# Two blocks of a fused fp32 transformer kernel: an earlier transpose, a first operand pair split in two, a last output in two parts

## The reference

```python
for i in range(2):
    mod = (c_act @ mod_w[i] + mod_b[i])           # six vectors of 1024
    hin = x * (1 + mod[1]) + mod[0]
    y = mla_mixer(hin) if i == 0 else moba_mixer(hin)
    x = layer_norm(ALPHA * x + mod[2] * y)
    hin = x * (1 + mod[4]) + mod[3]
    y = conv_ffn(hin)                             # 1024 -> 2 x 2816 -> 1024
    x = layer_norm(ALPHA * x + mod[5] * y)
```

## Time and profile before

| | |
|---|---|
| median of 3 runs | 892.44 us |
| profiled execution | 892.48 us |
| its span, first to last instruction | 890.6 us |
| TensorE matmuls | 857.5 us busy, 5768 instructions |
| VectorE | 668.7 us busy, 1090 instructions |
| ScalarE | 452.5 us busy, 720 instructions |
| GpSimd | 68.0 us busy, 62 instructions |
| mean granted TensorE clock | 0.997 |

### The profile page before, as it was taken

How to read it: one execution, slowest core, us unless ns; L and a number is a source line. 1 busy time by engine, 2 the same in 40 slices (tenths; PEclk the granted TensorE clock), 3 DMA queues, 4 the chain that set the end, 5 groups by cost and what they waited for, 6 DMA issues and landing times.

```text
span 890.6 us, 14511 instructions
## 1 busy us (share of the span) xinstructions
PE 857.5 (96%) x5768; PEld 754.0 (85%) x5768; DVE 668.7 (75%) x1090; ACT 452.5 (51%) x720; POOL 68.0 (8%) x62
## 2 busy tenths in 40 slices
PE   8999989999999999999999999899999999999996
PEld 8988978767876898699999999579987899999995
DVE  5598798878976997789757857796777876556557
ACT  5564554454546545275544545265563664444450
POOL 1000001000001120011200100110000111001011
PEclk9999999999999999999999999999999999999999
DMA  9756666555965780799866896389717886646601
GB/s 342 291 165 192 206 234 219 189 165 196 346 222 233 251 293 1 316 332 380 286 228 216 284 351 238 99 268 332 230 47 287 295 300 198 205 164 190 190 1 48
DMA packets 57028, 201.00 MB, mean 226 GB/s; under 512 B 6600, under 2 KB 7936, under 8 KB 56960
## 3 DMA queue, kind: packets, MB, share of 16 engines
q1 hardware_dynamic: 55952, 196.89, 63.2%
q0 software_dynamic: 1008, 3.18, 1.2%
HBM read 198.96 MB, written 1.08 MB: 225 GB/s over the span
## 4 chain that ended last, share of the span: by engine, by line
PE 81%; DVE 11%; ACT 4%; issue 2%; POOL 1%; DMA 0%; DVEq 0%
PE ps L1165 26%; PE ps L1166 25%; PE ps L1167 25%; DVE R L1476 2%; DVE wsp L1413 1%; PE ps L1178 1%; ACT pb L2116 1%; DVE wk L1451 1%; PE ps L1342 1%; PE ps L1381 1%; PE ps L1257 1%; DVE small L1854 0%; PE ps L1350 0%; PE ps L1357 0%; DVE X L1849 0%
## 5 line engine op out<-in xcount | busy, mean ns | idle before, releaser
L1165 PE MATMUL ps<-XT,wsp 128*128 128x256 f32 x768 | 217.1, 283 | 4.3 <-DVE XT L1458 3.0
L1166 PE MATMUL ps<-XT,wsp 128*128 128x256 f32 x768 | 214.5, 279 | 0.0
L1167 PE MATMUL ps<-XT,wsp 128*128 128x256 f32 x768 | 214.2, 279 | 0.0
L1413 DVE TENSOR_TENSOR wsp<-ring,wsp 128x1024 fp32r<-128x1024 f32 x144 | 178.7, 1249 | 9.3 <-ACT wsp L1958 9.3
L1958 ACT CAST wsp<-ring 128x1024 fp32r<-128x1024 f32 x143 | 148.6, 1045 | 61.9 <-PE ps L1167 54.7
L1165 PEld LDWEIGHTS ps<-XT,wsp 128*128 128x128 f32 x768 | 144.0, 187 | 8.5 <-issue 3.9
L1166 PEld LDWEIGHTS ps<-XT,wsp 128*128 128x128 f32 x768 | 144.0, 188 | 1.0
L1167 PEld LDWEIGHTS ps<-XT,wsp 128*128 128x128 f32 x768 | 143.7, 187 | 0.0
L1165 PE MATMUL ps<-wsp,ra 128*128 128x512 f32 x236 | 94.3, 400 | 4.0 <-issue 1.5
L1167 PE MATMUL ps<-wsp,ra 128*128 128x512 f32 x236 | 93.5, 396 | 0.0
L1166 PE MATMUL ps<-wsp,ra 128*128 128x512 f32 x236 | 93.3, 395 | 0.0
(11 more groups left out here) (272 smaller groups left out, 1517.7 us busy)
## 6 DMA issues: line engine op xcount, KB each, us to landing
arena<-in_mod_w SPq DMA_DIRECT2D x50, 512.0 KB, 6.2
ring<-in_mod_w SPq DMA_DIRECT2D x42, 512.0 KB, 4.9
ring<-in_ffn_a SPq DMA_DIRECT2D x28, 512.0 KB, 5.0
ring<-in_ffn_b SPq DMA_DIRECT2D x28, 512.0 KB, 5.1
arena<-in_ffn_o SPq DMA_DIRECT2D x22, 512.0 KB, 4.7
ring<-in_ffn_o SPq DMA_DIRECT2D x22, 512.0 KB, 4.8
arena<-in_ffn_a SPq DMA_DIRECT2D x16, 512.0 KB, 5.3
arena<-in_ffn_b SPq DMA_DIRECT2D x16, 512.0 KB, 4.9
```

Of the source, the lines that this page charges most:

```text
L1165: pe.matmul(o, l[0], r[0], start=start, stop=False)
L1166: pe.matmul(o, l[0], r[1], start=False, stop=False)
L1167: return pe.matmul(o, l[1], r[0], start=False, stop=stop)
L1413: ve.tensor_tensor(w[:, 1024:1024 + n], raw[slot[0]][:, 0:n], w[:, 0:n].bitcast(f32), SUB).then_inc(*done("V", "lo", u, also=[("raw", *slo ...
```

## The change

1. The rotated keys' two units are written out. The first one's 24 matmuls run as before; of the second one 12 run (k = 0 to 3), then the 8 transposes of c_q and c_kv with their ScalarE and VectorE steps, then the other 12, then "rope". The step "blk" gets the range of k.
2. In every transposing of kind "m" the pair k = 0 is handled by halves and its rest comes first: VectorE scales half 0 and half 1, ScalarE rounds each half as soon as it is scaled, VectorE takes the rest of each half; only then does VectorE scale pair 2. Its order becomes: scale 0, rest 0 (twice 256 wide), scale 2, scale 4, rest 2.
3. `ffn(i)` takes its banks when the first "fo" comes, not at its start. In the second layer the last 512 columns of t = 1 are two parts of 256 in two banks (five in all). Each part has its own product, sum and bn_stats, 256 wide; statistics of t = 1 there are taken over four groups of 256. The last operations of t = 0 stay behind (t = 1, columns 0 to 511), those of t = 1 behind the last part.

```diff
             m, ends = j % 2, j % per == per - 1 or j == blocks - 1
             full = m == 1 or j == blocks - 1
-            add("blk", x, nk, u, p, j % per, b, prior("bank", b), m, full, ends)
+            add("blk", x, nk, u, p, j % per, b, prior("bank", b), m, full, ends, range(nk))
...
                 pending.append((k, s))
-                if len(pending) > 1:
+                if len(pending) > 1 or k == 0:
                     low_part()
...
-    def resid(r, i, t, cb, b):
+    def resid(r, i, t, q, n, b):
+
         W.finish(gn[0])
         until(i, 5 if r else 2)
+        ends = 256 * q + n == 1024
         s = wk.get()
-        add("res_m", r, i, t, cb, b, s, prior("wk", s))
+        add("res_m", r, i, t, q, n, b, s, prior("wk", s))
...
-        add("res_a", r, i, t, cb, s)
+        add("res_a", r, i, t, q, n, s)
         wk.put(s[0])
-        add("res_s", r, i, t, cb)
-        if cb:
+        add("res_s", r, i, t, q, n)
+        if ends:
             add("res_z", r, i, t)
             for c in range(2 if final else 0):
                 add("out_g", t, c, final[0])
-        if final and t == 1:
+        if final and t == 1 and (q == 0 or ends):
             for c in range(2):
-                add("out", cb, c, final[1])
+                add("out", int(ends), c, final[1])
 
     def ffn(i):
-        outs = [[bank.get() for _ in range(2)] for _ in range(2)]
+
+        outs = []
         held, hold = [], {}
 
         def second(u):
+            if not outs:
+                outs.extend((t, q, n, bank.get()) for t, q, n in (
+                    (0, 0, 512), (0, 2, 512), (1, 0, 512), *(((1, 2, 256), (1, 3, 256)) if i else ((1, 2, 512),))))
             g = held.pop(0)
             for e in range(2):
                 w = W.next(f"ffn_o{i}", 2 * u + e)
-                for t in range(2):
-                    for cb in range(2):
-                        o = outs[t][cb]
-                        add("fo", i, u, t, e, cb, w, g, o, prior("bank", o), False, t == 1 and cb == 1)
+                for t, q, n, o in outs:
+                    add("fo", i, u, t, e, q, n, w, g, o, prior("bank", o), False)
                 W.done(w[1])
...
-            for cb in range(2):
+            for part in outs[2:]:
                 for j in js[len(free):]:
-                    piece(1, cb, j)
+                    piece(part, j)
...
-    proj_b("m00", 8, "mla_kr", 0, 2, lambda j, b: rope("kr", b))
+    b = bank.get()
+    u, p = W.next("mla_kr", 0)
+    add("blk", "m00", 8, u, p, 0, b, prior("bank", b), 0, False, True, range(8))
+    W.done(p)
+    u, p = W.next("mla_kr", 1)
+    add("blk", "m00", 8, u, p, 0, b, None, 1, False, False, range(4))
     transposed("cq", 4, "s", ks=(2, 0))
+    add("blk", "m00", 8, u, p, 0, b, None, 1, True, True, range(4, 8))
+    rope("kr", b)
+    bank.put(b[0])
+    W.done(p)
...
@@ vector @@
+                        if k == 0 and i == 0:
+                            ins.then_inc(*done("V", "xt_f0", tag))
...
                     tag, k, s = a
+                    if k == 0:
+                        for i in range(2):
+                            for e in new("V", ("xt_hi", tag, 0, i)):
+                                ve.wait_ge(*e)
+                            ve.tensor_tensor(XT[1][i], wk[s[0]][:, i * 256:(i + 1) * 256], XT[0][i].bitcast(f32),
+                                             SUB).then_inc(*done("V", "xt", tag, i, also=[("wk", *s)] if i else []))
+                        continue
...
+                    w = 256 if t and r and i else 512
+                    for c in range(q * 256, q * 256 + n, w):
+                        g = c // w * 6
+                        ins = ve.bn_stats(st[t][:, g:g + 6], X[:, t, c:c + w])
+                    ins.then_inc(*done("V", "res_s", r, i, t, q))
...
@@ scalar @@
+                    for i in range(2 if k == 0 else 0):
+                        for e in new("A", ("xt_f", tag, 0) if i else ("xt_f0", tag)):
+                            ac.wait_ge(*e)
+                        ac.copy(XT[0][i], wk[s[0]][:, i * 256:(i + 1) * 256]).then_inc(*done("A", "xt_hi", tag, 0, i))
+                    if k == 0:
+                        continue
```

More of the change, by code:

```diff
@@ L257, in proj_a @@
                 got = [W.next(name, base + cb * nq + q + e) for e in range(m)]
-                for t in range(2):
-                    add("row", x, nk, got, q, t, bs[t], prior("bank", bs[t]), q + m == nq)
+                for t, b in enumerate(bs):
+                    add("row", x, nk, got, q, t, b, prior("bank", b), q + m == nq)
                     if q + m == nq:
-                        evac(t, cb, bs[t])
-                        bank.put(bs[t][0])
+                        evac(t, cb, b)
+                        bank.put(b[0])
                 q += m
@@ L1199, in tensor @@
                 elif kind == "blk":
-                    x, nk, u, p, j, b, before, m, full, ends = a
+                    x, nk, u, p, j, b, before, m, full, ends, ks = a
                     w = parts[p[0]]
-                    for k in range(nk):
+                    for k in ks:
                         for e in new("P", ("lo", u), ready(x, k), before):
@@ L1234, in tensor @@
                     gh, gl = gp[g[0]][:, 0:512], gp[g[0]][:, 512:1024]
[L1235 to L1238, removed]
+                    c, cs = slice(e_ * 256 + t * 128, e_ * 256 + (t + 1) * 128), slice(q * 256, q * 256 + n)
+                    ins = mm3(ps[b[0]][:, 0:n], (gh[:, c], gl[:, c]), (parts[p[0]][:, 0:1024][:, cs],
+                                                                       parts[p[0]][:, 1024:2048][:, cs]),
+                              u == 0 and e_ == 0, k1)
+                    freed = ([("part", *p)] + ([("gp", *g)] if e_ else [])) if t == 1 and 256 * q + n == 1024 else []
                     if k1:
@@ L1836, in vector @@
                 elif kind == "res_m":
-                    r, i, t, cb, b, s, before = a
+                    r, i, t, q, n, b, s, before = a
                     for e in new("V", ("fill", *b), ("mod", i, 5 if r else 2), before):
                         ve.wait_ge(*e)
-                    ve.tensor_tensor(wk[s[0]], ps[b[0]], R2[:, r, cb * 512:(cb + 1) * 512], MUL).then_inc(
-                        *done("V", "res_m", r, i, t, cb,
-                              also=[("bank", *b)] + ([("r2", r)] if (i, t, cb) == (0, 1, 1) else [])))
+                    ve.tensor_tensor(wk[s[0]][:, 0:n], ps[b[0]][:, 0:n], R2[:, r, q * 256:q * 256 + n], MUL).then_inc(
+                        *done("V", "res_m", r, i, t, q,
+                              also=[("bank", *b)] + ([("r2", r)] if (i, t, q) == (0, 1, 2) else [])))
@@ L1843, in vector @@
                 elif kind == "res_a":
[L1844 to L1847, removed]
+                    r, i, t, q, n, s = a
+                    x = X[:, t, q * 256:q * 256 + n]
+                    tag, g = (("g0", 0), ("g1", 1), ("g2", 1), ("g3", 1))[2 * i + r]
+                    for e in new("V", ("res_m", r, i, t, q), ("gain", tag, g, t)):
@@ L1848, in vector @@
                         ve.wait_ge(*e)
-                    ve.tensor_tensor(x, x, wk[s[0]], ADD).then_inc(*done("V", "res_a", r, i, t, cb, also=[("wk", *s)]))
+                    ve.tensor_tensor(x, x, wk[s[0]][:, 0:n], ADD).then_inc(
+                        *done("V", "res_a", r, i, t, q, also=[("wk", *s)]))
                 elif kind == "res_s":
-                    r, i, t, cb = a
-                    for e in new("V", ("res_a", r, i, t, cb)):
+                    r, i, t, q, n = a
+                    for e in new("V", ("res_a", r, i, t, q)):
@@ L1858, in vector @@
                     m = mv2[:, t * 4:t * 4 + 4]
-                    for e in new("V", ("res_s", r, i, t, 0), ("res_s", r, i, t, 1)):
+                    for e in new("V", [("res_s", r, i, t, q) for q in ((0, 2, 3) if t and r and i else (0, 2))]):
                         ve.wait_ge(*e)
-                    ve.bn_aggr(m[:, 0:2], grid(st[:, t * 12:(t + 1) * 12], 2)).then_inc(*done("V", "res_v", r, i, t, 0))
+                    ve.bn_aggr(m[:, 0:2], grid(st[t], 4) if t and r and i else grid(st[t][:, 0:12], 2)).then_inc(*done("V", "res_v", r, i, t, 0))
                     for e in new("V", ("res_v", r, i, t, 0)):
```

36 lines of the change are left out of this document (17 added, 19 removed).

## The result

The changed kernel takes 896.65 us (median of 9 runs, 893.64 to 899.36), the kernel before beside it 892.72 us (9 runs): ratio 1.004, interval 1.0024 to 1.0055 (here and below the ratio is of the means of the runs, so it can differ a little from that of the medians). Slower by 3.9 us. The forecast was 892.1 us, the range 890.6 to 893.7: the measured time lies 3 us above it. The profiled execution took 896.3 us, its span 894.5.

A forecast was written before the change was run, and what follows sets the result against it. TensorE was taken as the bound, busy 96% of the span, with VectorE holding some stretches. Terms -0.40, +0.31, -0.70, +0.31, +0.1, +0.02 sum to -0.36 us against 892.48; with the median 0.04 lower, 892.1 us, range 890.6 to 893.7.

The forecast's parts named there:

- the other 0.9 turns into TensorE waiting in the MLA heads: Of TensorE's 1.30 us lead at the value projection, 0.40 stays; the rest becomes waiting for VectorE in the MLA heads.
- m00 and the keys, -0.40: First mixer's transposing plus rotated keys: value projection 1.30 us earlier, of which 0.40 us stays; bounds +0.31 and -2.46.
- m01 and m11, +0.31 each: Feed-forward transposings: first wait moves to k = 2, rest 2 comes late, 0.31 us lost each; m01 bounds -1.5, +0.62.
- m10, -0.70: Second layer's mixer transposing: first wait gained, 0.70 us, weight stream covering it with 1.06 slack; bounds -0.73 and 0.
- The tail, +0.02: Kernel's end: halved last part saves nothing because VectorE is behind at the last fill, +0.02 us; bounds -0.8 and +0.5.
- The matmuls, +0.1: Last 512 columns split in two: 66 more matmuls cost 0.1 us; bounds nothing and 0.15.
- (d): Rival: VectorE's 0.31 us delay counts in all four transposings, +1.36 us in all, 893.8 us; chance 0.11.
- rival b: First wait counts everywhere: m01 and m11 gain 0.98 us each instead of losing 0.31, 889.5 us; chance 0.08.
- (a): Rival: TensorE's 1.30 us lead survives the MLA heads, another 0.9 off, 891.2 us; chance 0.13.
- (c): Rival: the tail gains what it halves, VectorE free at the last fill, 0.8 us less, 891.3 us; chance 0.09.
- (e): Rival: the earlier key transposes do nothing because c_q comes too late, only if after 301.5 us; chance 0.02.
- three signs by which I would have been wrong: m01's k = 2 under 3.9 us after first scale; MLA heads keeping the lead; VectorE idling before the last fill.

The follow-up runs named there:

- the last table: Fillers (unread matmuls) in long TensorE waits: split in mixers only 889.98 us, whole change 890.57, kernel before 891.84; kernel before without fillers 892.98.
- part 3 alone: Kernel before with only the last 512 columns in two parts, banks taken late: 893.33 us, ratio 1.0 (0.9988 to 1.0013).
- the pair of the third job with four places filled: Whole change and kernel before, both with fillers including one in the sparse-attention heads, the change also in m01 and m11: 893.72 and 894.01 us.
- The kernel with the split in the mixers alone: Changed kernel with first pair split only in m00 and m10, fillers at mLSTM, MLA and m10: 889.98 us, ratio 0.9966 to the kernel before.
- part 1 alone: Kernel before with only the earlier transposes of c_q and c_kv, banks taken late: 893.33 us, ratio 1.0006 (0.9992 to 1.002).
- the three kernels with three places filled: Mixers-only split, whole change (also filled in m01 and m11) and kernel before, fillers at mLSTM, MLA and m10: 889.98, 890.57, 891.84 us.

## Why the prediction was wrong

**The step that failed** is in part 2: "The first wait merely moves to k = 2, and TensorE goes on 0.31 later", and in the keys' part "the other 0.9 turns into TensorE waiting in the MLA heads". Both were right as schedule. Both priced a wait at its length: I held two waits of 0.98 and 0.52 equal to one of 1.79 less 0.29, and one of 0.80 made longer a matter of where time is spent. A wait that gets longer can also cost TensorE's clock, 1.36 to 1.63 us each time here, 4.5 us in all, and no term or rival of mine had that: the sum put it at nothing. Over all profiles without a filler at the place, the wait of 1.78 to 1.80 us lost the clock at five of its six places (three profiles), the pair of 0.98 and 0.52 at none of twenty (ten profiles). The MLA heads' wait of 1.57 lost it in six of seven, the one of 0.80 in none of three. The trace of before held the hint: PEclk 0.83 in 120 to 130 us, behind the 2.26 us wait at 122.35, which none of my rows showed, since I read windows only as busy shares. The clock row of the page hides it: each digit is a fortieth of the span, over 22 us, and a stretch of 3.4 us still gives a 9.

The Trainium skill (TensorE: Matmul & The Clock Gate, "What's actually happening") says that TensorE's clock has two states, 1.2 and 2.4 GHz, and that the chip picks by how busy the array has lately been. The two levels agree with the rows above (0.50 and 1.00). The case of falls in a kernel under its heading "HAM oscillation — how this bites in real kernels" is a wait for DMA ahead of every tile, longer than any wait here; in this kernel waits of 1.44, 1.57 and 1.79 us between dense matmuls were enough in some runs. The measurement decides.

**m00 and the keys, -0.40: the size right, the way there only in part.** TensorE's first product starts at 283.57, 1.04 earlier (0.98 forecast); VectorE's rest 2 at 285.65, 0.31 later, as forecast. But m00's lead was not lost ahead of the transposes of c_q, where I had put it ("waits for VectorE: m00's gain is given back here"). Most of it went at the third weight unit. The changed kernel there:

```profile
288.61 1.22 DVE L1427 TENSOR_TENSOR wsp<-ring,wsp 128x1024 fp32r<-128x1024 f32 x1
...
289.88 0.50 PE L1178 MATMUL ps<-wsp,XT 128*128 128x512 f32 x1 [0.36 <-DVE wsp L1427]
```

and the kernel before:

```profile
288.29 1.22 DVE L1413 TENSOR_TENSOR wsp<-ring,wsp 128x1024 fp32r<-128x1024 f32 x1
...
290.29 0.39 PE L1165 MATMUL ps<-wsp,XT 128*128 128x512 f32 x1
```

The unit's rest starts 0.32 later, TensorE is there early and waits, and from 0.93 its lead goes to 0.41 at this matmul and to 0.31 at the next. That is VectorE's delay showing as a wait for a weight. Then the timeline around the keys:

```profile
299.31 0.88 DVE L1912 TENSOR_SCALAR arena<-ps,small 128x256 f32<-128x256 f32 x2 [0.82 <-POOL small L2351]
...
299.84 1.38 PE L1191 MATMUL ps<-cst,arena 128*128 128x128 f32 x8
...
300.98 0.37 PE L1178 MATMUL ps<-XT,ra 128*128 128x256 f32 x1
...
302.48 0.39 PE L1178 MATMUL ps<-wsp,ra 128*128 128x512 f32 x1
```

VectorE's write ends at 300.19 (forecast 300.18). The transposes start at 299.84, before that end: those that read token half t = 0 go first. No wait stands ahead of them, where I had expected about 1 us. So the value projection starts 1.57 earlier, not 1.30. What the result hangs on came as forecast: VectorE starts the first weight rest behind this place at 305.08 instead of 305.04 (0.05 late forecast), and at the long wait of the MLA heads the lead is 0.38.

**m01 and m11, +0.31 each: right** (+0.30 and +0.29 in the table). VectorE's part of m01:

```profile
378.18 1.00 DVE L1465 TENSOR_SCALAR wk<-ps,small 128x256 f32<-128x256 f32 x2 [0.86 <-PE ps L1191]
...
379.20 0.88 DVE L1476 TENSOR_TENSOR XT<-wk,XT 128x256 fp32r<-128x256 f32 x2
...
379.99 1.90 DVE L1465 TENSOR_SCALAR wk<-ps,small 128x256 f32<-128x256 f32 x4
...
381.80 0.68 DVE L1481 TENSOR_TENSOR XT<-wk,XT 128x512 fp32r<-128x512 f32 x1
```

Rest 2 starts 3.62 after the first scale (3.64 forecast, 3.33 before), TensorE's k = 2 at 4.36 (4.37 by the forecast's steps, 4.06 before). With fillers it can be seen alone: from m01's transposes to its k = 2, 4.80 us with the split (375.77 to 380.57) and 4.51 without (375.71 to 380.22). Twice 0.29 is the 0.59 between the two medians of the last table, though their intervals overlap.

**m10, -0.70: right**, 0.81 in the table, 0.08 beyond the larger bound; its cover held.

**The tail, +0.02: right.** VectorE has no gap, as the forecast said:

```profile
884.92 1.40 DVE L1975 SCALAR_TENSOR_TENSOR X<-X,small,ring 128x512 f32<-128x512 f32 x2
886.23 0.42 DVE L1863 TENSOR_TENSOR wk<-ps,R 128x256 f32<-128x256 f32 x1
...
888.39 0.43 DVE L1881 BATCH_NORM_STATS2 small<-X 128x6 f32<-128x256 f32 x1
```

From the product that starts at 882.80 to the end of this last bn_stats, 888.82, are 6.02 us; before, from 878.97 to 884.99, as much.

**The matmuls, +0.1: not visible.** From m11's transposes to the end part 3 alone takes 198.05 us (695.25 to 893.3) and the kernel before 198.16, so tail and matmuls together cost nothing that these profiles show.

**The sum** of -0.36 stands against -0.6 in the profiles, and -1.3 between the medians of the change and of before, both with fillers. The last is less sure than it looks: the fillers are not the same in both (the change has 12 matmuls in the MLA heads and 14 each in m01 and m11, the kernel before 5 and none), and the two profiled executions stand the other way round, 889.4 and 888.4. Of that 1.0 us, 0.9 lies ahead of the first place that the change touches: m00's transposes start at 278.21 and 277.29. From there to the end the two take 611.2 and 611.1 us, and the pair of the third job with four places filled 610.7 (the change) and 611.1. So what the schedule of the whole change gains lies between nothing and 0.4 us in the traces, which fits the forecast. The kernel with the split in the mixers alone takes 610.0.

**The rivals.** (d) was the slower one, and VectorE's place in line did cost what it said in m01 and m11; in m00 it took back 0.62 of TensorE's lead without changing what was left at the MLA heads, and in m10 nothing. The slowdown isn't its. The Trainium skill's sentence on breaking up instructions (rival b) held for the first wait alone, as weighed: the instruction queued behind the halves was late by 0.31 us, and the next wait took over. (a), (c) and (e) did not occur, nor did any of the three signs by which I would have been wrong: they look at the schedule, and none looks at the clock.

**What stays open.** Which long wait loses the clock in a given run: waits of 1.44, 1.57, 1.79, 2.27 and 2.33 us did in some executions and not in others, and I found no row ahead of them that tells it. That part 1's longer MLA wait adds its share in the whole change rests on the stretch at 332 us, in six of seven profiles with the longer wait; by itself part 1 measured no different.

## What to carry to other kernels

When a change removes a short wait of TensorE but hands it to the next wait, price the merged wait by what the granted clock does behind it, not by its length: read the clock in windows of 2 us behind every wait over a microsecond, in several executions. Where a wait can't be taken away, a few matmuls without a reader, in a bank that is free at once and placed at the wait itself, kept the clock in every profile here and cost nothing that shows; a filler that itself waits for a bank did not (the clock fell in all three profiles) and held up real work. And split work for latency only where the first piece feeds enough work to cover the second: in the mixers it did (2.8 us), in the feed-forward parts it did not (0.7 us).

## What the runs showed of the hardware

- TensorE's granted clock went to 0.50 for 3.4 us at waits of 1.44 to 2.36 us, and once behind two of 0.72 and 0.85. The fall began between 0.2 us before the end of the wait and 1.5 us after it. It cost 1.36 to 1.63 us in the changed kernel, and about 0.8 at 578 us in the run with the first pair whole (from m01's transposes to m11's 316.78 us, in part 1 alone without a fall 315.99).
- Two like waits (1.78 and 1.79 us) in one execution were followed by 1.00 and by 0.61 in the next windows. With it goes most of the spread of one kernel's times (890.94 to 896.42 us for part 1 alone, at clocks 0.999 and 0.993), while the three kernels with three places filled spread over 1.4 to 3.5 us.
- Splitting a rest of 512 columns in two costs VectorE about 0.2 us more (0.88 for two against 0.68 to 0.69 for one), and 256-wide product, sum and bn_stats took 0.42, 0.42 and 0.43 where 512 wide took 0.68 to 0.69.
